# Differential attention of the prompt: the bias moves from VectorE to TensorE, the row-sum scaling moves to the head norm, and the PSUM slots and the order of products change

## The reference, cut to what matters

```
s = einsum('bqhmd,bkhmd->bhmqk', q, k) * DK**-0.5          # two maps m of width 64 per head
bias = rel_bias[rel_bucket(kpos - qpos)]                    # per head, by distance
visible = (kpos // 64) <= (qpos // 64)
p = softmax(where(visible, s + bias, -inf))
attn = p[:, :, 0] - lam * p[:, :, 1]
o = einsum('bhqk,bkhd->bqhd', attn, v)                      # head width 128
y_att = rmsnorm(o, subln_w) * (1 - lam_init)                # norm over the 128 of a head
```

## Time and profile before

| | us |
|---|---|
| median of 3 runs | 1885.67 (1883.65 to 1889.14) |
| the profiled execution | 1889.13 |
| its span, first to last instruction | 1887.3 |
| attn_prompt, first scores to last output copy | 587.5 to 749.7 |
| head norm, first sum to last logarithm | 827.1 to 839.7 |

### The profile page before, as it was taken

One profiled execution on the slowest core, in us unless ns is written; L12 is line 12 of the kernel. 1 busy time (PEld: TensorE's weight loads), 2 busy tenths in 40 slices (PEclk: granted clock), 3 DMA queues, 4 the chain that ended last, 5 costly groups with the idle time before them and its releaser, 6 DMA issues. The chain is left out here.

```text
span 1887.3 us, 23502 instructions
## 1 busy us (share of the span) xinstructions
PE 1667.1 (88%) x9183; PEld 1462.5 (77%) x9183; DVE 1042.4 (55%) x1808; ACT 624.3 (33%) x1089; POOL 444.1 (24%) x270
## 2 busy tenths in 40 slices
PE   4489998779997887757986999999999999999896
PEld 2378987669995555535776999999988888989775
DVE  1665515860015998444344766666556677667744
ACT  1422212211112444343232322222444445444532
POOL 0331111113220000006544333333361101111132
PEclk8789999979996889887997999999999999999998
DMA  8545110112213000623561221221236434454342
GB/s 278 189 149 168 34 36 1 45 51 58 70 59 128 1 1 1 203 100 94 196 221 56 79 67 56 68 68 57 88 100 182 134 108 136 135 168 123 135 155 76
DMA packets 164563, 192.25 MB, mean 102 GB/s; under 512 B 7858, under 2 KB 126875, under 8 KB 164416
## 3 DMA queue, kind: packets, MB, share of 16 engines
q1 hardware_dynamic: 139626, 132.11, 22.8%
q10 hardware_dynamic: 19612, 40.93, 6.7%
q0 software_dynamic: 5216, 17.71, 2.7%
HBM read 173.62 MB, written 17.11 MB: 101 GB/s over the span
## 5 line engine op out<-in xcount | busy, mean ns | idle before, releaser
L556 PE MATMUL PS<-h_hi,weights_hi 128*128 128x384 f32 x1280 | 437.1, 341 | 10.5 <-POOL h_lo L2079 5.8
L2066 POOL TENSOR_TENSOR weights_lo<-weights_raw,weights_hi 128x1024 fp32r<-128x1024 f32 x99 | 253.5, 2561 | 788.7 <-ACT weights_hi L1657 764.7
L557 PE MATMUL PS<-h_lo,weights_hi 128*128 128x384 f32 x1280 | 434.5, 339 | 0.0
L558 PE MATMUL PS<-h_hi,weights_lo 128*128 128x384 f32 x1280 | 434.3, 339 | 0.0
L1657 ACT ACTIVATE weights_hi<-weights_raw 128x1024 fp32r<-128x1024 f32 x202 | 213.6, 1058 | 221.0 <-PE PS L982 105.0
L556 PEld LDWEIGHTS PS<-h_hi,weights_hi 128*128 128x128 f32 x1280 | 244.4, 191 | 17.4 <-issue 12.6
L557 PEld LDWEIGHTS PS<-h_lo,weights_hi 128*128 128x128 f32 x1280 | 244.4, 191 | 0.0
L558 PEld LDWEIGHTS PS<-h_hi,weights_lo 128*128 128x128 f32 x1280 | 244.0, 191 | 0.0
L980 PE MATMUL PS<-weights_hi,g_hi 128*128 128x512 f32 x396 | 160.8, 406 | 15.0 <-DVE weights_lo L1604 12.7
L2194 POOL TENSOR_TENSOR g_lo<-g_T,g_hi 128x384 fp32r<-128x384 f32 x66 | 81.7, 1239 | 372.5 <-ACT g_hi L1961 372.5
L981 PE MATMUL PS<-weights_lo,g_hi 128*128 128x512 f32 x396 | 158.9, 401 | 0.0
(11 more groups left out here) (355 smaller groups left out, 2493.2 us busy)
## 6 DMA issues: line engine op xcount, KB each, us to landing
weights_raw<-in_w_up_dram SPq DMA_DIRECT2D x88, 512.0 KB, 3.9
weights_raw<-in_w_down_dram SPq DMA_DIRECT2D x66, 512.0 KB, 4.4
w_ada_unit<-in_w_ada_dram SPq DMA_DIRECT2D x32, 512.0 KB, 5.7
weights_raw<-in_w_in_dram SPq DMA_DIRECT2D x24, 512.0 KB, 4.2
weights_raw<-in_w_out_dram SPq DMA_DIRECT2D x24, 512.0 KB, 3.8
w_ada<-in_w_ada_dram SPq DMA_DIRECT2D x4, 2048.0 KB, 16.1
k_cache<-in_cache_k_dram ACTq DMA_DIRECT2D x8, 1024.0 KB, 5.2
x_scratch<-x_new POOLq DMA_DIRECT2D x9, 512.0 KB, 5.8
```

What stands on the lines that cost most here:

```text
L556: pe.matmul(out, wh, xh, start=(i == 0), stop=False)
L557: pe.matmul(out, wh, xl, start=False, stop=False)
L558: mm = pe.matmul(out, wl, xh, start=False, stop=(i == n - 1))
L2066: mark(gp.tensor_tensor(WL[n % 3][:, :], WR[:, n % 3, :], WH[n % 3][:, :].bitcast(F32), ALU.subtract), "w_lo")
```

## The change

- **Bias.** A block's scores are no longer touched by VectorE. The bias table is split into a float32r high part BH and a float32r rest BL, and TensorE adds both to the scores in PSUM by products with an identity matrix in float32r (`IDR`), 128 columns at a time: 2 maps x 2 column groups x 2 parts = 8 products per block (4 for block 0 of a head). They have the full 128 rows. VectorE makes IDR, BH and BL at the start of the stage.
- **Score slots.** Three slots of two banks (banks 0 to 5) instead of two. Map m of block s uses slot (2s+m) mod 3. Both maps of block s now wait for one event: the exponential of map 0 of block s-1.
- **Alternation.** For each 512 columns, map 0 and map 1 follow each other.
- **Turned attn.** It has one bank (6) instead of two, so blocks with i >= 4 are turned and copied in two pieces. TensorE makes the second piece after the values of block s-3. The output has one bank (7).
- **Row sum.** `attn` is now exp0 + (-lambda l0/l1) exp1, without the division by the first row sum l0: one small and one long operation less. The row norm cancels a factor of a row except in its epsilon, so the head norm gets an extra term DV*EPS*(l0^2-1), added by four float32 products per tile (a broadcast column of `EL` against the identity).
- **Output copy.** `o_T` is copied out by ScalarE.
- ScalarE's order is exp map 0, first piece of block s-2, exp map 1, output s-4, second piece of s-2.

The core of the diff:

```
 def scores(s):                                    # TensorE
-    for m in range(2):
-        if s >= 1: pe.wait_ge(sem("exp"), 2 * (s - 1) + m + 1)
-        for c0 in range(0, W, 512):
-            mm = pe.matmul(PS[:, 2 * m + c0 // 512, ...], QT[m ...], KTT[m ...], start=True, stop=True)
-        mm.then_inc(sem("scores"), 1)
+    if s >= 1: pe.wait_ge(sem("exp"), 2 * s - 1)
+    S = [2 * ((2 * s + m) % 3) for m in range(2)]
+    for c0 in range(0, W, 512):
+        for m in range(2):
+            pe.matmul(PS[:, S[m] + c0 // 512, ...], QT[m ...], KTT[m ...], start=True, stop=c1 <= lo)
+    for m in range(2):
+        for b0 in range(lo, W, P):
+            pe.matmul(out, IDR[:, :], BH[:, h, at_b:at_b + P], start=False, stop=False)
+            mm = pe.matmul(out, IDR[:, :], BL[:, h, at_b:at_b + P], start=False, stop=...)
+        mm.then_inc(sem("scores"), 1)
...
+for s in range(NBK + 3):
+    if s < NBK: scores(s)
+    if 2 <= s < NBK + 2: attn_turn(s - 2, 0)      # waits attn, attn_T of the piece before
+    if s >= 3: attn_values(s - 3)                 # waits attn_T
+    if 2 <= s < NBK + 2 and blocks[s - 2][1] >= 4: attn_turn(s - 2, 1)
...
 for i in range(NT):                               # TensorE, head norm
-    pe.matmul(PS[:, i % 2, :], C("ones"), SQ[:, i % 2, :], start=True, stop=True)
+    pe.matmul(PS[:, i % 2, :], C("ones"), SQ[:, i % 2, :], start=True, stop=False)
+    for q in range(4):
+        mm = pe.matmul(PS[:, i % 2, q * P:(q + 1) * P], EL[:, row:row + 1].to_broadcast([P, P]), ident, ...)
...
 def combine(s):                                   # VectorE
-    ch(ve.reciprocal(RL[:, 0:2], LS[...]))
-    ch(ve.tensor_scalar(RL[:, 1:2], RL[:, 1:2], LAM[:, 2:3], None, ALU.mult))
-    ch(ve.tensor_scalar(PR[:, q, 1, 0:W], PR[:, q, 1, 0:W], RL[:, 1:2], None, ALU.mult))
-    out(ve.scalar_tensor_tensor(out=ATT[...], in0=PR[:, q, 0, 0:W], scalar=RL[:, 0:1], in1=PR[:, q, 1, 0:W], ...))
+    ch(ve.reciprocal(RL[:, q:q + 1], LS[:, q:q + 1]))
+    ch(ve.scalar_tensor_tensor(out=RL[:, q:q + 1], in0=L1[:, s:s + 1], scalar=LAM[:, 2:3], in1=RL[:, q:q + 1], ...))
+    out(ve.scalar_tensor_tensor(out=ATT[...], in0=PR[:, q, 1, 0:W], scalar=RL[:, q:q + 1], in1=PR[:, q, 0, 0:W], ...))
...
-        ch(ve.tensor_tensor(S[:, lo:W], S[:, lo:W], BIASP[...], ALU.add))
...
-        out(ve.tensor_copy(OT[:, h, i * P:(i + 1) * P], PS[:, 6 + t % 2, 0:P]), "o_out")
...
+def o_rows_out(t):                                # ScalarE
+    mark(ac.activation(OT[:, h, i * P:(i + 1) * P], PS[:, 7, 0:P], ACT.Copy), "o_out")
```

More of the change, by code:

```diff
@@ L230, in build @@
     ATB = [r("attn_T_a", [P, D])]
+    IDR = r("ident_r", [P, P], F32R)
+    BIASP = at("bias_prompt", [P, NH, 256], R1)
     ATB.append(at("attn_T_b", [P, D], xr_off))
@@ L437, in build @@
         LATE_SECTIONS = [2, 5, 3, 4]
+        PIECES = [sum(1 + (u % NPT >= 4) for u in range(t)) for t in range(NH * NPT + 1)]
         PAIRS_AT_NORM = [2, 4, 6, 8]
@@ new lines, in _, with scores @@
+            NBK = len(blocks)
+            def scores(s):
+                h, i = blocks[s]
+                W = (i + 1) * P
+                lo = max(0, W - 2 * P)
+                if s >= 1:
+                    pe.wait_ge(sem("exp"), 2 * s - 1)
+                S = [2 * ((2 * s + m) % 3) for m in range(2)]
+                for c0 in range(0, W, 512):
+                    c1 = min(W, c0 + 512)
+                    for m in range(2):
+                        pe.matmul(PS[:, S[m] + c0 // 512, 0:c1 - c0], QT[m * DK:(m + 1) * DK, h, i * P:(i + 1) * P],
+                                  KTT[m * DK:(m + 1) * DK, h, c0:c1], start=True, stop=c1 <= lo)
+                for m in range(2):
+                    for b0 in range(lo, W, P):
+                        out = PS[:, S[m] + b0 // 512, b0 % 512:b0 % 512 + P]
+                        at_b = 2 * P - W + b0
+                        pe.matmul(out, IDR[:, :], BH[:, h, at_b:at_b + P], start=False, stop=False)
+                        mm = pe.matmul(out, IDR[:, :], BL[:, h, at_b:at_b + P], start=False,
+                                       stop=b0 + P == W or (b0 + P) % 512 == 0)
+                    mm.then_inc(sem("scores"), 1)
@@ new lines, in attn_turn, with attn_values @@
+            def attn_turn(t, piece):
+                h, i = blocks[t]
+                pe.wait_ge(sem("attn"), t + 1)
+                if PIECES[t] + piece >= 1:
+                    pe.wait_ge(sem("attn_T"), PIECES[t] + piece)
+                for k in range(4 * piece, min(i + 1, 4 * piece + 4)):
+                    mm = turn(PS[:, 6, (k % 4) * P:(k % 4 + 1) * P], ATT[:, t % 2, k * P:(k + 1) * P])
+                mm.then_inc(sem("attn_turned"), 1)
+            def attn_values(t):
+                h, i = blocks[t]
+                pe.wait_ge(sem("attn_T"), PIECES[t + 1])
+                if t >= 1:
+                    pe.wait_ge(sem("o_out"), t)
+                for k in range(i + 1):
+                    mm = pe.matmul(PS[:, 7, 0:P], VTOK[:, k, h * DV:(h + 1) * DV],
+                                   ATB[t % 2][:, k * P:(k + 1) * P], start=(k == 0), stop=(k == i))
+                mm.then_inc(sem("o"), 1)
@@ L817, in _ @@
+            for s in range(NBK + 3):
+                if s < NBK:
+                    scores(s)
+                if 2 <= s < NBK + 2:
+                    attn_turn(s - 2, 0)
+                if s >= 3:
+                    attn_values(s - 3)
+                if 2 <= s < NBK + 2 and blocks[s - 2][1] >= 4:
+                    attn_turn(s - 2, 1)
             phase_end(pe, "attn_prompt")
@@ L874, in _ @@
             for i in range(NT):
-                pe.wait_ge(sem("o_sq"), i + 1)
                 if i >= 2:
                     pe.wait_ge(sem("o_ln"), i - 1)
-                pe.matmul(PS[:, i % 2, :], C("ones"), SQ[:, i % 2, :], start=True, stop=True).then_inc(sem("o_sum"), 1)
+                pe.wait_ge(sem("o_sq"), i + 1)
+                pe.matmul(PS[:, i % 2, :], C("ones"), SQ[:, i % 2, :], start=True, stop=False)
+                for q in range(4):
+                    h, j = divmod(4 * i + q, NT)
+                    row = h * NPT + j if j < NPT else NH * NPT
+                    mm = pe.matmul(PS[:, i % 2, q * P:(q + 1) * P], EL[:, row:row + 1].to_broadcast([P, P]), ident,
+                                   start=False, stop=q == 3)
+                mm.then_inc(sem("o_sum"), 1)
             def yn_turn(j):
@@ L1289, in _ @@
             ve.wait_ge(*once("bias_turned"))
-            ch(ve.tensor_copy(BIASP[:, 0:2, :], PS[:, 0, :].rearrange("p (h n) -> p h n", h=2)))
+            mark(ve.tensor_copy(BIASP[:, 0:2, :], PS[:, 0, :].rearrange("p (h n) -> p h n", h=2)), "dve_step")
+            mark(ve.tensor_copy(IDR[:, :], C("ident")), "dve_step")
+            mark(ve.tensor_copy(BIASS[:, :], PS[:, 2, 0:144]), "dve_step")
             ch(ve.tensor_copy(BIASP[:, 2:4, :], PS[:, 1, :].rearrange("p (h n) -> p h n", h=2)))
-            ch(ve.tensor_copy(BIASS[:, :], PS[:, 2, 0:144]))
-            out(ve.tensor_tensor(BIASP[:, :, P:2 * P], BIASP[:, :, P:2 * P],
-                                 C("future").unsqueeze(1).to_broadcast([P, NH, P]), ALU.add), "dve_once")
+            ch(ve.tensor_tensor(BIASP[:, :, P:2 * P], BIASP[:, :, P:2 * P],
+                                C("future").unsqueeze(1).to_broadcast([P, NH, P]), ALU.add))
+            ch(ve.tensor_copy(BH[:, :, :], BIASP[:, :, :]))
+            out(ve.tensor_tensor(BL[:, :, :], BIASP[:, :, :], BH[:, :, :].bitcast(F32), ALU.subtract), "dve_once")
             PSF = PS[:, :, :].rearrange("p b n -> p (b n)")
@@ L1303, in combine @@
                 ve.wait_ge(sem("exp"), 2 * (s + 1))
-                ch(ve.reciprocal(RL[:, 0:2], LS[:, 2 * q:2 * q + 2]))
-                ch(ve.tensor_scalar(RL[:, 1:2], RL[:, 1:2], LAM[:, 2:3], None, ALU.mult))
-                ch(ve.tensor_scalar(PR[:, q, 1, 0:W], PR[:, q, 1, 0:W], RL[:, 1:2], None, ALU.mult))
+                ch(ve.reciprocal(RL[:, q:q + 1], LS[:, q:q + 1]))
+                ch(ve.scalar_tensor_tensor(out=RL[:, q:q + 1], in0=L1[:, s:s + 1], scalar=LAM[:, 2:3],
+                                           in1=RL[:, q:q + 1], op0=ALU.mult, op1=ALU.mult))
                 if s >= 2:
[L1308 to L1312, removed]
+                    ve.wait_ge(sem("attn_turned"), PIECES[s - 1])
+                out(ve.scalar_tensor_tensor(out=ATT[:, q, 0:W], in0=PR[:, q, 1, 0:W], scalar=RL[:, q:q + 1],
+                                            in1=PR[:, q, 0, 0:W], op0=ALU.mult, op1=ALU.add), "attn")
+            for s in range(NBK + 1):
                 if s < NBK:
@@ L1812, in _, with exps @@
             NBK = len(blocks)
-            for s in range(NBK + 2):
-                if s < NBK:
[L1815 to L1818, removed]
-                    for m in range(2):
[L1820 to L1831, removed]
+            def exps(s, m):
+                W, q = (blocks[s][1] + 1) * P, s % 2
+                if s >= 2:
+                    ac.wait_ge(sem("attn"), s - 1)
```

(26 more changed lines are left out.)

52 lines of the change are left out of this document (12 added, 40 removed).

## The result

The changed kernel takes 2000.07 us (median of 4 runs, 1993.66 to 2004.9), the kernel before 1884.66 in the same comparison: a ratio of 1.061, 95% interval [1.057, 1.064]. The forecast was 1880 us. The profiled execution has a span of 1998.5 us, 111.2 more than before. By stages: attn_prompt, from the first scores to the last value product, 161.7 us before and 264.5 after (+102.8); from there to the head norm 77.8 and 82.5 (+4.7); the head norm 12.6 and 19.3 (+6.7); the rest -3.0. So nearly all of it is in the one stage where a gain of 12.6 us was forecast.

A forecast was written before the change was run, and what follows sets the result against it. VectorE was taken as the bound, busy 139.4 of attn_prompt's 162.2 us. The stage's -12.6 us and the head norm's +7.0 gave -5.6 on the median of 1885.67, about 1880 us; range 1869 to 1898.

The forecast's parts named there:

- a gain of 12.6 us: Stage attn_prompt: start +2.3 us, heads 1 and 2 -8.6 less 0.4, head 3 -3.6, tail -0.8; sum -12.6.
- The new loop: Attention blocks: scores(s) waits for exp(s-1, map 0); L(i) = 1.5 + 0.453(i+1) us; steps sum to 34.3 us a head, against 37.4.
- Two things lie across it.: Across the loop: TensorE's in-order turns and values of earlier blocks; second turn awaiting the copied first piece, 0.75 to 0.9 us.
- exp, output, piece, exp: ScalarE's order in the last step of a head, from i = 7 to the next i = 0, put at 3.1 us.
- Waits add up: Rival: 0.15 to 0.2 us more per step from queues not seen before, +6 us, so 1886; chance 0.14.
- if turns wait long for ScalarE's copies: Last-named sign of being wrong, after two-record bias products and a clock near 0.85; no size given.
- The tail: Stage end after the last block's first exponential: 10.6 us before, 9.8 after, -0.8.
- Bias products 0.112 us apart: TensorE's float32r bias products: spacing 0.112 us, four per map 0.45 us, 0.90 a block.
- both rivals on their price: Bias products dear, 0.224 us each: 1899, chance 0.17; or cheap, 0.058 us each: 1871, chance 0.12.
- The clock: Full clock in heads 1 to 3; rival: half clock for a quarter of their time, +8 us, 1888, chance 0.12.
- Maps side by side in either order: Score products: both maps overlap, 0.213 us per 128 columns, alternation free; rival without overlap +31 us, 1911, chance 0.03.
- Head norm: Four added float32 products per tile, eight records 0.112 us apart, 0.90 us at full clock; +7.0 us, nothing covers it.

The follow-up runs named there:

- copy-first kernel: The changed kernel with ScalarE copying the output of block s-4 before the first exponential of block s instead of after the second; 1884.84 us, ratio to before 1.0004.
- one-bank kernel: The kernel before with one output bank instead of two, nothing else of the change; 1997.93 us (one run).

## Why the prediction was wrong, step by step

**What failed** is in "The new loop": "Two things lie across it." There was a third. TensorE's value products of block s-3 wait for the output copy of s-4, and that one is behind both exponentials in ScalarE's order. The prediction counted the values as TensorE's work and put their wait at nothing, without a reason, although the single output bank is in the list of changes above it. It also had ScalarE's order right: its "exp, output, piece, exp" for the step from i = 7 to 0 is the end of a round and the start of the next. It did not follow the changed count of the wait on `o_out` through that order. The copy was priced at 8.5 us of ScalarE's time and nothing for being late.

**What the runs showed in its place**: the values waited 69.7 us for the copy, and with the copy first the stage is 113.3 us shorter (264.5 to 151.2) and the median 115 us (2000.07 to 1884.84). No rival named this wait. "Waits add up" had the place, ScalarE's one order, and 6 us; among the signs of being wrong, "if turns wait long for ScalarE's copies" came nearest, but it was the values that waited. The copy-first kernel is close to what the prediction had in fact summed, and the one-bank kernel shows that this wait alone makes the old stage 113.9 us longer.

**The terms otherwise**, measured in the copy-first kernel. Head 1 step by step, from first exponential to first exponential: 3.82, 4.48, 4.15, 3.79, 4.24, 4.69, 5.95, 3.52, in sum 34.6; forecast 3.85, 4.55, 4.2, 3.8, 4.2, 4.7, 5.9, 3.1 and 34.3. In the last step ScalarE was through its order after 3.2 us, near the forecast 3.1, but then waited for a row maximum. Its scores came behind TensorE's second turn, which had waited for the copied piece:

```profile
656.97 0.41 PE L507 MATMUL PS<-CONST,attn 128*128 128x128 f32 x2 [1.23 <-ACT attn_T_b L1862]
...
658.65 0.37 ACT L1853 ACTIVATE probs<-PS,row_max 128x128 f32<-128x128 f32 x1 [0.29 <-DVE row_max L1359]
```

The sum of the stage looks better than it was. From the first scores to the last output copy this kernel takes 151.5 us where the old one takes 162.1, a gain of 10.6. But the forecast gain of 12.6 had already paid 2.3 us for the new work at the start of the stage, which lies ahead of the first scores and measured 1.9 (from the first copy of the bias to the last operation ahead of the scores 4.4 us instead of 2.5). Like for like the gain is 8.7, and 3.9 us are missing. Head 2 gained 2.4 instead of 4.3, since the clock fell in its first step (granted 0.60 over 658.7 to 663.0; 5.42 us instead of 3.82). The tail grew by 0.3 us instead of shrinking by 0.8. Head 3 gained 2.9 instead of 3.6, and that is a slip of the sum: it compared 34.8 us between the ends of two exponentials of different length with 31.2 between two starts; between starts it is 34.0 before.

- Bias products 0.112 us apart: right, so both rivals on their price fall. The Trainium skill, "TensorE: Matmul & The Clock Gate", section on weight-path perf modes, would have made their load a quick one. It does not show here: the loads of the bias products last 0.19 us, as those of plain float32 in the earlier trace rows. The 56 ns that the prediction took from the section on the issue gap is its figure for an isolated product; for a stream with loads the same section gives about 81 ns, and 112 were measured.
- The clock: 1.00 in heads 1 to 3 but for the one step above, as taken. That rival falls for this kernel, though in the change itself the clock fell to 0.67 behind the new idle time.
- Maps side by side in either order: right. The stretch that it was read from, 3.38 us for W = 896, was not all at half clock (granted 0.59 over 727.2 to 730.6); in a row the maps would still take 5.1 us at that clock, so the reading holds.
- Head norm: 19.1 us, +6.5 against before; the added products cost 7.0, as forecast, none hidden.

**What stays open.** Against the kernel before, the copy-first kernel should lose 1.9 us at the start of the stage, gain 10.5 in it and lose 6.5 in the norm: 2.1 us faster. The medians are equal (0.7 us slower, the interval from 1.1 faster to 2.4 slower). In its profile three stretches in which the code is the same differ by more than that: 2.9 us shorter ahead of the stage, 2.5 longer between the stage and the norm, 7.1 shorter behind the norm. Such differences appear between other runs too (77.2 to 82.5 us between stage and norm), so the missing 1 to 4.5 us can't be placed.

## What to carry to other kernels

When a buffer goes from two copies to one, its wait moves one round earlier: list for every such wait where its release stands in the releasing engine's order, and what that engine must do first. A late release that costs nothing with two buffers can put two engines in series. And when no engine is busy and the clock is low, look at the first wait of the engine that feeds the others. Here the low clock was a consequence of it.

## What the runs showed of the hardware that was not expected

A float32r product with 128 x 128 weights took 0.112 us with 128 columns and 0.12 with 256, so up to 256 columns are nearly free here; and going from products on 64 rows to products on 128 cost about 0.15 us on the path (starts 0.21 and 0.16 us apart instead of 0.11). The granted clock followed the order of one copy: 0.67, 0.84 and 0.93 as it moved ahead of one and then of both exponentials, with the same work on every engine.
